# Matmuls by identity, whose results nothing reads, in TensorE's waits, and latent attention's squares ahead of a table load

## Time and profile before

| what | value |
|---|---|
| median of 3 runs | 3207.59 us (3201.6 to 3207.85) |
| the profiled execution's own time | 3191.56 us |
| its span, first to last instruction | 3189.8 us |
| its mean granted TensorE clock | 0.978 |
| PE, matmul | 3010.5 us busy, 15406 instructions |
| DVE | 1876.6 us busy |
| ACT | 953.8 us busy |
| POOL | 809.0 us busy |
| DMA | 170 MB, 53 GB/s over the span |

### The profile page before, as it was taken

The page is one execution under the profiler, slowest core; times in us unless marked ns, Lnnn a source line. Parts: engine busy times, 40 slices in busy tenths (PEclk is TensorE's granted clock), DMA queues, the critical chain, the costliest instruction groups (busy, mean ns, idle before and its releaser), DMA issues. The chain is left out here.

```text
span 3189.8 us, 38699 instructions
## 1 busy us (share of the span) xinstructions
PE 3010.5 (94%) x15406; PEld 2425.4 (76%) x15406; DVE 1876.6 (59%) x2777; ACT 953.8 (30%) x1840; POOL 809.0 (25%) x466
## 2 busy tenths in 40 slices
PE   7999998888999999999899999999998999999888
PEld 6777787767788888888677777777686777777667
DVE  4333666534754154254579898888534466776773
ACT  3332344324211000011333333334212344444431
POOL 3121000241433333333223333332142221111111
PEclk9998999989999999999999999999999999999899
DMA  3002000010111111112211212114131100000021
GB/s 127 34 34 96 14 1 14 29 65 20 66 52 47 46 51 48 53 50 69 86 41 47 79 41 80 51 69 169 56 98 66 40 27 34 27 27 27 8 79 66
DMA packets 49275, 170.27 MB, mean 53 GB/s; under 512 B 5200, under 2 KB 5472, under 8 KB 48224
## 3 DMA queue, kind: packets, MB, share of 16 engines
q1 hardware_dynamic: 49120, 168.15, 14.9%
HBM read 145.06 MB, written 23.07 MB: 53 GB/s over the span
## 5 line engine op out<-in xcount | busy, mean ns | idle before, releaser
L194 PE MATMUL acc<-x_hi,w_hi 128*128 128x512 f32 x2048 | 830.6, 406 | 54.8 <-POOL w_lo L189 23.8
L187 POOL CAST w_hi<-w_raw 128x1024 fp32r<-128x1024 f32 x217 | 239.6, 1104 | 2327.3 <-PE acc L196 1390.2
L196 PE MATMUL acc<-x_hi,w_lo 128*128 128x512 f32 x2048 | 806.9, 394 | 0.0
L195 PE MATMUL acc<-x_lo,w_hi 128*128 128x512 f32 x2048 | 806.8, 394 | 0.0
L189 POOL TENSOR_TENSOR w_lo<-w_raw,w_hi 128x1024 fp32r<-128x1024 f32 x217 | 549.1, 2530 | 17.4
L194 PEld LDWEIGHTS acc<-x_hi,w_hi 128*128 128x128 f32 x2048 | 390.3, 191 | 151.8 <-issue 45.1
L196 PEld LDWEIGHTS acc<-x_hi,w_lo 128*128 128x128 f32 x2048 | 389.9, 190 | 84.0
L195 PEld LDWEIGHTS acc<-x_lo,w_hi 128*128 128x128 f32 x2048 | 390.7, 191 | 79.0 <-issue 2.4
L2550 DVE SCALAR_TENSOR_TENSOR acc<-ev_upad,cols,acc 128x1024 f32<-128x1024 f32 x232 | 298.5, 1286 | 5.4
L194 PE MATMUL aux<-x_hi,w_hi 128*128 128x512 f32 x464 | 197.5, 426 | 0.6 <-POOL w_lo L189 0.6
L196 PE MATMUL aux<-x_hi,w_lo 128*128 128x512 f32 x464 | 183.4, 395 | 0.0
(11 more groups left out here) (507 smaller groups left out, 4947.2 us busy)
## 6 DMA issues: line engine op xcount, KB each, us to landing
w_raw<-in_stream SPq DMA_DIRECT2D x217, 512.0 KB, 3.4
h<-in_x SPq DMA_DIRECT2D x16, 512.0 KB, 9.0
spill_h<-h SPq DMA_DIRECT2D x8, 512.0 KB, 5.3
spill<-ev_zst SPq DMA_DIRECT2D x8, 512.0 KB, 4.0
h_even<-spill_h SPq DMA_DIRECT2D x8, 512.0 KB, 12.3
ev_bz<-spill SPq DMA_DIRECT2D x8, 512.0 KB, 3.5
spill_h<-h_even SPq DMA_DIRECT2D x8, 512.0 KB, 5.3
h<-spill_h SPq DMA_DIRECT2D x8, 512.0 KB, 4.4
```

Source lines behind the costliest of these rows:

```text
L187: pool.tensor_copy(k.w_hi[slot][:], k.w_raw[slot][:]).then_inc(k.w_split, 1)
L194: pe.matmul(out, w_hi, x_hi, start=start, stop=False)
L195: pe.matmul(out, w_hi, x_lo, start=False, stop=False)
L196: return pe.matmul(out, w_lo, x_hi, start=False, stop=stop)
```

## The change

A helper `keep_warm(k, pe, out, n)` issues n matmuls of the bf16 identity by itself, 128x128, into 128 columns of PSUM, with no semaphore. It is called on PE:

- behind the ones-matmuls of `HalfNorm.on_tensor`, 28 (even and diff);
- behind `first_two`, 50 (even and diff);
- at the end of PE's stream in mix (48), in cross attention (45), in FFN (45) and in even (45);
- in the first query tile's first half, 30 ahead of the wait for row 0 and 12 ahead of each of the rows 1 to 7;
- in cross attention ahead of the wait for the last head's queries, 30, and ahead of the loop over token tiles, 40;
- in latent attention ahead of the wait for the squares, 30, and 2 in each of the 8 turns of the sums;
- in diff attention, for head 6 and t below 5, 8 in each `quarter`, of t == 0 only in the last, behind a wait for all copies of the streamed tiles: 17 groups, 136 matmuls.

That makes 705. And at the start of latent attention the squares of `projA`'s tiles 1 and 2 are issued on ACT ahead of the table load, the square of tile 0 on DVE as a multiplication. What is computed stays the same.

```diff
--- before.py
+++ after.py
@@ -196,6 +196,12 @@
     return pe.matmul(out, w_lo, x_hi, start=False, stop=stop)
 
 
+def keep_warm(k, pe, out, n):
+
+    for _ in range(n):
+        pe.matmul(out, k.ident_h, k.ident_h, start=True, stop=True)
+
+
 def linear_tile(k, pe, n, slot, turn, x_hi, x_lo, kt, width=SEQ, ready=None):
 
     pe.wait_ge(k.w_split, n * 2 + 2)
@@ -334,6 +340,7 @@
         pe.wait_ge(self.early.summed, KD - 1)
         for c in (0, HALF):
             pe.matmul(self.k.aux[:, c:c + HALF], self.k.ones, self.early.acc[:, c:c + HALF], start=True, stop=True).then_inc(self.total, 1)
+        keep_warm(self.k, pe, self.k.aux[:, 3 * HALF:3 * HALF + P], 28)
 
     def root_of(self, act, c):
         cols = slice(c * HALF, (c + 1) * HALF)
@@ -384,6 +391,7 @@
                               norm.x_hi[:, q, cols], norm.x_lo[:, q, cols], q == 0, q == KD - 1)
                 if q == KD - 1:
                     mm.then_inc(k.lin_done if c else half, 1)
+    keep_warm(k, pe, k.aux[:, 3 * HALF:3 * HALF + P], 50)
 
 
 class Split:
@@ -716,6 +724,7 @@
                     feed(1)
                 turn(TT - 1)
             assert at[0] == 8 * N_IN
+            keep_warm(k, pe, A[:, 0:P], 48)
 
         @block.scalar
         def _(act):
@@ -975,6 +984,7 @@
             for c in (0, HALF):
                 for i in range(KD):
                     if j == 0 and c == 0:
+                        keep_warm(k, pe, acc[:, 0, HALF:HALF + P], 12 if i else 30)
                         pe.wait_ge(norm.ready[0], norm.ready[1] + i + 1)
                     mm = product3(pe, acc[:, slot_of(j), c:c + HALF], k.w_hi[n % 2][:, i * P:(i + 1) * P], k.w_lo[n % 2][:, i * P:(i + 1) * P],
                                   x_hi[:, i, c:c + HALF], x_lo[:, i, c:c + HALF], i == 0, i == KD - 1)
@@ -1024,6 +1034,8 @@
                 pe.wait_ge(s["exped"], 4 * (t - 1))
             for h in range(XA_HEADS):
                 if t == 0:
+                    if h == XA_HEADS - 1:
+                        keep_warm(k, pe, acc[:, 0, h * MEM:h * MEM + P], 30)
                     pe.wait_ge(s["q_normed"], h + 1)
                 mm = pe.matmul(acc[:, t % 2, h * MEM:(h + 1) * MEM], q[:, h, t * P:(t + 1) * P], kk[:, h, :], start=True, stop=True)
             mm.then_inc(s["scores"], 1)
@@ -1031,6 +1043,7 @@
         scores(0)
         scores(1)
         pe.wait_ge(s["v_copied"], 1)
+        keep_warm(k, pe, aux[:, SEQ:SEQ + P], 40)
         for t in range(TT):
             pe.wait_ge(s["normed"], t + 1)
             if t:
@@ -1050,6 +1063,7 @@
                     mm = pe.matmul(aux[:, SEQ + (t % 2) * HALF + h * P:SEQ + (t % 2) * HALF + (h + 1) * P],
                                    v[:, m, h * P:(h + 1) * P], pT[:, t % 2, m * HALF + h * P:m * HALF + (h + 1) * P], start=m == 0, stop=m == 1)
             mm.then_inc(s["done"], 1)
+        keep_warm(k, pe, aux[:, 0:P], 45)
 
     def on_scalar(act):
         norm.root_of(act)
@@ -1365,8 +1379,10 @@
                     mm = pe.transpose(acc[:, j % 2, t * P:(t + 1) * P], o_tok[:, t, j * P:(j + 1) * P], k.ident)
                 mm.then_inc(s["o_turned"], 1)
 
+            keep_warm(k, pe, aux[:, 3 * HALF:3 * HALF + P], 30)
             pe.wait_ge(s["squares"], 3)
             for t in range(TT):
+                keep_warm(k, pe, aux[:, 3 * HALF:3 * HALF + P], 2)
                 for q in range(2):
                     pe.matmul(aux[:, t:t + 1], square[:, q, t * P:(t + 1) * P], k.ones[:, 0:1], start=q == 0, stop=q == 1)
                 mm = pe.matmul(aux[:, TT + t:TT + t + 1], square[:, 2, t * P:(t + 1) * P], k.ones[:, 0:1], start=True, stop=True)
@@ -1448,9 +1464,9 @@
 
         @block.scalar
         def _(act):
+            for q in range(1, 3):
+                act.activation(square[:, q, :], projA[:, q, :], ACT.Square).then_inc(s["squares"], 1)
             load_log_exp(act)
-            for q in range(3):
-                act.activation(square[:, q, :], projA[:, q, :], ACT.Square).then_inc(s["squares"], 1)
             for q in range(4):
                 act.activation(m_hi[:, q, :], mixg[:, q, :], ACT.Copy).then_inc(s["g_hi"], 1)
 
@@ -1542,6 +1558,7 @@
         @block.vector
         def _(dve):
             step = Steps(dve, s["chain"])
+            dve.tensor_tensor(square[:, 0, :], projA[:, 0, :], projA[:, 0, :], ALU.mult).then_inc(s["squares"], 1)
             dve.wait_ge(s["squares"], 3)
             for q, g in enumerate((COLS["qa_norm"], COLS["qa_norm"] + 1, COLS["kva_norm"])):
                 dve.tensor_scalar(projA[:, q, :], projA[:, q, :], k.cols[:, g:g + 1], None, ALU.mult).then_inc(s["gained"], 1)
@@ -1815,6 +1832,7 @@
                     over_tiles(pe, ga[p], da[p], tile(x_hi, x_lo, KD))
                 late_tile(da[p], g_hi, g_lo, tiles, s["lo"], first[p])
                 over_tiles(pe, da[p] + 1, da[p] + KD, tile(g_hi, g_lo, tiles))
+            keep_warm(k, pe, k.aux[:, 0:P], 45)
 
         @block.scalar
         def _(act):
@@ -3037,6 +3056,10 @@
                 def quarter(n):
                     if fill:
                         part(h + 2, t // 2, t % 2, range(2 * n, 2 * n + 2))
+                    elif not pieces and (t or n == 3):
+                        if t == 0:
+                            pe.wait_ge(s["copied"], 8 * H)
+                        keep_warm(k, pe, aux[:, 0:P], 8)
                     if n in (0, 3):
                         for m in pieces[n // 3:n // 3 + 1]:
                             piece(m)
```

## The result

| | before | after |
|---|---|---|
| median, first comparison (7 runs each) | 3206.25 us (3201.6 to 3207.85) | 3183.41 us (3179.49 to 3193.52) |
| ratio, 95% interval | | 0.9939 (0.9929 to 0.995) |
| profiled execution: own time, span, clock | 3191.56, 3189.8 us, 0.978 | 3183.37, 3181.6 us, 0.987 |

The change makes the kernel 0.6% faster. The medians differ by 22.8 us but the two profiled executions by 8.2 us only: the first thing to explain.

The account below looks back on a forecast made before the run. TensorE, busy for 94% of the span at a mean clock of 0.978, was taken as the bound. Terms summed to -14.65 us, from 3207.6 to 3193, stated as 3192 us; range 3178 to 3202.

Parts of the forecast that it names:

- the carry-over to the median: Timed median 16 us above the profiled execution; executions said to differ by 0.5%, so the difference was kept in the forecast.
- may fall differently: About half a dozen cold stretches without fillers stay, and may fall differently; no size or sign given.
- all is held: Rival: the sums and every joint stay warm, best bounds together -25 us, 3183 us; chance 0.16.
- Mix to latent attention: Joint and sums of squares: opens 0.9 us later, PE starts 1.3 us earlier net, sums gain 1.3; -2.6 us.
- Query tile: First query tile behind the norm: PE warm, gaining from 664.29 on where it alone is on the path; -2.4 us.
- Cross scores: Cross attention's scores and transposes: warm, transposes start 0.9 us earlier, 4.95 us behind them become about 2.8; -3.0 us.
- Cross to FFN: Joint of cross attention and FFN: opens 1.15 us later, the cold work behind gives back 1.6; -0.45 us.
- Even: Even block: -1.9 us at the FFN-to-even joint and norm, -1.6 us behind its first two tiles.
- Diff: Even-to-diff joint and norm: same gain as the FFN-to-even joint, whose rows it repeats; -1.9 us.
- Unfilled head: Head of diff attention, 17 groups of 8 fillers: VectorE mostly the bound, small gain of -0.8 us, bounds -1.5 and +3.
- price of a filler: Identity matmuls on PE: 57 ns apart at full clock, 0.11 us at the lower level; bounds 57 and 98 ns.
- slower rival: Matmuls by identity do not hold the clock, so groups in cold places run at 0.11 us each: +9.2, 3217 us; chance 0.06.

Follow-up runs that it names:

- third version: Kernel after, without head fillers or those in the sums' turns, some joint groups resized, more waits filled, against the kernel before: 3167.46 us, ratio 0.9879.
- no query and cross: Kernel after without the fillers of the first query tile, the cross scores and the head, against the kernel before: 3185.94 us, ratio 0.9954.

## Why the prediction was right, and where it was not

It said faster, 3192 us in 3178 to 3202; the result is 3183.4, 8.6 us below the forecast.

**The step that failed: the carry-over to the median.** "I carry the difference over to the median" took the 16 us between the profiled execution and the median for noise that stays. It is a cold stretch of 24 us in the last head of latent attention, worth 10.8 us, absent from the one profile read and present in three others (46.1 to 46.3 us against 35.5), the second profile of the same kernel among them. In the 13 runs of the kernel after, four lie at 3188 us or more, the rest at 3177 to 3185. So the 22.8 us between the medians look like two parts: the fillers where they stand (12 us, below), and a fall that comes less often without being filled. The first is measured by stage. The second is inferred: both profiles of after lack the fall, and its four runs at 3188 us or more have the lower mean clocks (0.983 to 0.986 against 0.987 to 0.990), but none of them was profiled. It was in the text only as "may fall differently", without size or sign.

That the result is in the range is in part luck. The 12 us alone would have given 3194; what brought it to 3183, near the range's lower end, is a fall that the working has at nothing.

The time is that of the rival "all is held" (3183), but not for its reason: the sums fell, two joints fell, 17 cold stretches were left.

Term by term, between the two profiled executions:

- *Mix to latent attention*, -2.6: measured -2.9. The joint opens 0.83 us later (0.9 taken), the first sum 1.3 us sooner (1.3). From VectorE's end to the out-projection 16.52 us became 12.70; in the stretch behind it, cold until 276.5, 0.96 came back. "Four turns warm, four cold" was about right (the clock fell after some five), and so was the doubt that two fillers a turn hold the clock.
- *Query tile*, -2.4: -1.75. A fall came despite the fillers, at 645.2, 1.3 us into the first 30 of them, which stand behind a wait of 2.13 us for the weights; from 648.7 on the clock is 1.00, and the rows wait for VectorE 0.8 us as forecast.
- *Cross scores*, -3.0: -3.2 (0.92 before the transposes, 2.29 behind).
- *Cross to FFN*, -0.45: -0.4, from +1.13 and -1.52 (+1.15 and -1.6). Not counted: a fall at 764, which before did not have, +1.65.
- *Even*, -1.9 and -1.6: -1.2 and -1.6. *Diff*, -1.9: -2.3. In both joints the clock fell, at the end of the wait that stays open (even, 2.5 us) or 1.2 us behind it (diff, 2.7 us), and it cost little: in the third version it falls at neither, and even's stage is only 0.2 us shorter, diff's the same. VectorE sets the rows there.
- *Unfilled head*, -0.8: +1.3. The sign was wrong. The bound named the cause (groups ahead of scores that VectorE wants), and it should have been taken as the value, since VectorE is what ends last there.
- *The rest*, taken as 0: falls in heads 1 to 4 of diff and at the end moved about and cost the profiled execution 3.5 us net, the last head another 1.3; the start of mix, which has no edit, gained 2.7.

The filled places add up to -2.9-1.75-3.2-0.4-2.8-2.3+1.3 = -12.0 us, against -14.65. The other stages took 3.8 of them back, which leaves the 8.2 us between the two profiled executions. These 3.8 are 1.65 (the fall at 764), 1.3 (539), 3.5 (diff and the end), less 2.7 (the start of mix). The first may be a price of the fillers in the query tile and the cross scores (no query and cross did not have it); the prediction has nothing for it.

**The price of a filler** held: 56 ns at full clock, as the earlier trace rows gave (57). The Trainium skill (TensorE: Matmul & The Clock Gate, section Back-to-back issue gap) has about 81 ns for such a stream with weight loads. The rows of 45, 96, 100 and 140 contradict it here. The slower rival, that matmuls by identity do not hold the clock, fell: rows of 96, 100 and 140 of them ran 56 ns apart, at full clock, and the work behind the 100 too.

## What to carry to other kernels

Fill a wait of PE only where PE ends last behind it, end the group before the wait does, and at a block's end before the slowest other engine does: each filler past that costs its 56 ns in full. Look for small waits in dense stretches of small matmuls too; filling two of about a microsecond went with 8 us in the median, in one experiment. And profile the kernel before more than once when its profile is faster than its median: the difference is a place, and it can be found.

## What the runs showed that was not expected

- The last head can stay at 0.50 for 24 us with PE busy for all of 21.0 us, and the sums for 11.3 us; yet the same sums, entered warm, ran seven turns at 1.00 with nothing added (in the third version three). Work that does not bring the clock back may still run at full clock for a while. Which property of the work decides was not tried.
- One 2 us shift at 262 us moved most runs of the kernel from 3203 to 3192 us, by their clocks through the fall 280 us later. What sets the moment of a fall, beyond the waits, stays open.
- Medians of such a kernel are mixtures of groups (3192 and 3203), and differences of 5 us between kernels were hidden in them; stage lengths of single profiles told 0.1 us.
